# A three-layer fp32 model on one core: a new order for two merged attentions, and two weight-split steps moved

## What is computed

```python
# even mixer, after the projections; 8 heads each, causal, 512 tokens
mla = softmax(mask(q @ k.T * 96**-0.5)) @ v            # q, k of 96 columns, v of 64
z   = sq @ sk.T * 64**-0.5                             # stick-breaking, 64 columns
lb, l1 = log_sigmoid(z), where(k_idx < q_idx, log_sigmoid(-z), 0)
a   = where(k_idx < q_idx, exp(lb + reverse_cumsum(l1) - l1), 0)
sb  = a @ sv
o   = concat(mla, sb) @ w_o
```

## Time and profile before

| what | value |
|---|---|
| median of three runs | 2888.7 us |
| the profiled execution | 2887.3 us |
| its span | 2885.6 us |
| mean granted clock of TensorE in it | 0.939 |
| TensorE, VectorE, ScalarE, GpSimd busy | 2657.8, 1522.2, 1234.1, 122.6 us |

### The profile page before, as it was taken

One profiled execution on the slowest core, in us unless ns is written; L12 is line 12 of the kernel. 1 busy time (PEld: TensorE's weight loads), 2 busy tenths in 40 slices (PEclk: granted clock), 3 DMA queues, 4 the chain that ended last, 5 costly groups with the idle time before them and its releaser, 6 DMA issues. The chain is left out here.

```text
span 2885.6 us, 30599 instructions
## 1 busy us (share of the span) xinstructions
PE 2657.8 (92%) x12110; PEld 2158.0 (75%) x12110; DVE 1522.2 (53%) x2085; ACT 1234.1 (43%) x1570; POOL 122.6 (4%) x166
## 2 busy tenths in 40 slices
PE   6998999999998999999989969798995899999994
PEld 5866778888887777888877658677874777877774
DVE  4555444344323654434466443245346788888884
ACT  3366432223334742213222222324242677777773
POOL 0111000000140000000000000000002000000001
PEclk9967799999998999999989989899997899999997
DMA  3300132433431023342322022221304899999993
GB/s 130 119 1 1 50 120 93 139 109 119 138 110 37 1 76 116 108 146 88 117 88 88 30 95 88 73 88 59 142 14 190 345 392 396 395 396 396 396 392 119
DMA packets 157146, 432.84 MB, mean 150 GB/s; under 512 B 11051, under 2 KB 80838, under 8 KB 144582
## 3 DMA queue, kind: packets, MB, share of 16 engines
q1 hardware_dynamic: 148950, 400.90, 38.1%
q10 hardware_dynamic: 4608, 16.78, 1.4%
q0 software_dynamic: 3440, 13.11, 1.3%
HBM read 383.58 MB, written 47.19 MB: 149 GB/s over the span
## 5 line engine op out<-in xcount | busy, mean ns | idle before, releaser
L307 PE MATMUL ps<-area,area 128*128 128x512 f32 (+1 forms) x1696 | 658.5, 388 | 0.0
L330 DVE TENSOR_TENSOR area<-area,area 128x2048 fp32r<-128x2048 f32 (+4 forms) x161 | 340.5, 2117 | 598.5 <-ACT area L324 598.5
L306 PE MATMUL ps<-area,area 128*128 128x512 f32 (+5 forms) x1432 | 552.0, 385 | 0.0
L324 ACT ACTIVATE area<-area 128x2048 fp32r<-128x2048 f32 (+4 forms) x161 | 284.1, 1767 | 615.6 <-PE ps L307 582.4
L2324 DVE TENSOR_TENSOR area<-area,area 128x2048 fp32r<-128x2048 f32 x192 | 433.9, 2286 | 107.3 <-ACT area L2319 107.3
L305 PE MATMUL ps<-actT_parts,area 128*128 128x512 f32 x968 | 385.4, 398 | 11.6 <-DVE area L330 9.4
L306 PE MATMUL ps<-actT_parts,area 128*128 128x512 f32 x968 | 383.3, 396 | 0.0
L2319 ACT ACTIVATE area<-area 128x2048 fp32r<-128x2048 f32 x192 | 361.0, 1913 | 48.5 <-PE ps L2353 18.4
L307 PEld LDWEIGHTS ps<-area,area 128*128 128x128 f32 x1696 | 320.4, 189 | 68.3
L306 PEld LDWEIGHTS ps<-area,area 128*128 128x128 f32 x1432 | 277.5, 194 | 52.8
L305 PE MATMUL ps<-area,actT_parts 128*128 128x512 f32 (+3 forms) x704 | 274.6, 390 | 39.6 <-DVE area L330 30.8
(11 more groups left out here) (329 smaller groups left out, 3205.3 us busy)
## 6 DMA issues: line engine op xcount, KB each, us to landing
area<-in_w SPq DMA_DIRECT2D x96, 2048.0 KB, 10.1
area<-in_w_in SPq DMA_DIRECT2D x16, 2048.0 KB, 7.9
area<-in_l_w_gate SPq DMA_DIRECT2D x22, 1024.0 KB, 5.4
area<-in_l_w_up SPq DMA_DIRECT2D x22, 1024.0 KB, 8.0
expert_inputs<-maskz SPq DMA_DIRECT2D x39, 512.0 KB, 8.7
area<-in_l_w_in SPq DMA_DIRECT2D x9, 2048.0 KB, 8.2
area<-expert_inputs SPq DMA_DIRECT2D x32, 512.0 KB, 9.7
expert_rows<-area ACTq DMA_DIRECT2D x32, 512.0 KB, 8.6
```

The source lines that it names most:

```text
L306: pe.matmul(dst(r), a.l, b.h, start=False, stop=False)
L307: m = pe.matmul(dst(r), a.h, b.l, start=False, stop=end)
L324: eng.activation(w.h, raw, ACT.Copy).then_inc(w_hi, 1)
L330: dve.tensor_tensor(w.l, raw, w.high_f, ALU.subtract).then_inc(w_lo, 1)
```

## The change

No arithmetic is added or removed.

- In the merged attention the methods of class `Attention` are cut into steps (`pe_preps`, `pe_scores`, `pe_turn`, `pe_values`; `act_preps`, `act_copy`, `act_exp`; `dve_out`), as are those of stick-breaking, and the four loops call them in a new order. Iteration v now is, on TensorE: stick-breaking transposes of v - 3, its scores v, MLA preparations, stick-breaking values v - 5 (before v - 4), MLA scores v, MLA transposes v - 2, MLA values v - 4 (before v - 3). On ScalarE: absolute value and exponential v, copy v - 3, weights' exponential v - 2, logarithm v, MLA preparation copy, MLA copy v - 2, MLA exponential v. On VectorE: MLA output v - 5 (before v - 4), scan v - 1, stick-breaking output v - 5, subtraction v - 1, MLA maximum and bias v, stick-breaking log step v. On GpSimd: triangle of the weights v - 2 (before v - 1), triangle of the sums v.
- MLA has one score bank (0) in place of two, stick-breaking three (1, 3, 4) in place of two. `prep_bank` and `turn_banks` are not changed, both are bank 2. The wait of stick-breaking's scores for the subtraction of unit v - 2 is not changed.
- In the mixer `after` stands behind a job's second chunk.
- In the experts `turned_low` stands at q = p + 1.

The Fox and mLSTM attentions call the cut methods in the old order.

```diff
             def pe(self, pe, v):
+                self.pe_preps(pe, v)
+                self.pe_scores(pe, v)
+                self.pe_turn(pe, v - 2, v)
+                self.pe_values(pe, v - 3)
...
             mla = Attention(...
-                            score_banks=(0, 1), turn_banks=(2,), value_banks=(6,), prep_bank=2)
+                            score_banks=(0,), turn_banks=(2,), value_banks=(6,), prep_bank=2)
...
             def sb_bank(v):
-                return ps[:, 3 + v % 2, 0:causal(v)]
+                return ps[:, (1, 3, 4)[v % 3], 0:causal(v)]
...
             def two_po(po, ch):
-                for v in range(U0 + 1):
...
+                for v in range(U0 + 2):
+                    drop_weights(po, v - 2)
+                    drop_sums(po, v)
 
             def two_pe(pe, ch):
-                for v in range(U0 + 4):
-                    sb_pe(pe, v)
-                    mla.pe(pe, v)
+                for v in range(U0 + 5):
+                    sb_turn(pe, v - 3)
+                    sb_scores(pe, v)
+                    mla.pe_preps(pe, v)
+                    sb_values(pe, v - 5)
+                    mla.pe_scores(pe, v)
+                    mla.pe_turn(pe, v - 2, v)
+                    mla.pe_values(pe, v - 4)
 
             def two_act(act, ch):
                 act.preload_act_table_set("natural_log_exp_and_others")
                 for v in range(U0 + 3):
-                    sb_act(act, ch, v)
-                    mla.act(act, v)
+                    t1 = T1[:, v % 4, 0:causal(v)]
+                    if v < U0:
+                        act.wait_ge(b_sc, v + 1)
+                        if v >= 4:
+                            act.wait_ge(b_w, v - 3)
+                        ch(act.activation(t1, sb_bank(v), ACT.Abs))
+                        ch.mark(act.activation(t1, t1, ACT.Exp, scale=-1.0))
+                    powers = ch.n
+                    sb_copy(act, v - 3)
+                    sb_weights(act, v - 2)
+                    if v < U0:
+                        ch.wait(powers)
+                        act.activation(t1, t1, ACT.Ln, bias=1.0).then_inc(b_t1, 1)
+                    mla.act_preps(act, v)
+                    mla.act_copy(act, v - 2)
+                    mla.act_exp(act, v)
 
             def two_dve(dve, ch):
                 for v in range(U0 + 5):
-                    sb_dve(dve, ch, v)
+                    mla.dve_out(dve, ch, v - 5)
+                    sb_scan(dve, ch, v - 1)
+                    scanned = ch.n
+                    sb_out(dve, v - 5)
+                    sb_less(dve, ch, v - 1, scanned)
                     mla.dve(dve, ch, v)
+                    sb_logs(dve, v)
...
@@ mp_act, and the same in mp_dve @@
-                    if c % 4 == 3:
+                    if c % 4 == 1:
                         msp.after(act, at_qk[j])
...
@@ ex_dve @@
-                        if q == p + 2:
+                        if q == p + 1:
                             turned_low(dve, n)
```

More of the change, by code:

```diff
@@ L880, in pe, with pe_scores @@
                         m.then_inc(s_pr, 1)
-                if self.mlstm and v < units and v % NT == 0:
+            def pe_scores(self, pe, v):
+                nsc = len(self.sc_banks)
+                if self.mlstm and v < self.units and v % NT == 0:
                     if v:
@@ L943, in act, with dve_out @@
                                        accum_out=col(rs, v)).then_inc(s_ex, 1)
[L945 to L949, removed]
+            def dve_out(self, dve, ch, u):
+                if 0 <= u < self.units:
                     h, i = divmod(u, NT)
@@ L954, in dve @@
                     dve.tensor_scalar(self.dst(h, i), self.value_at(u), col(rinv, u), None, ALU.mult).then_inc(s_on, 1)
-                    last = False
+            def dve(self, dve, ch, v):
+                units, mlstm, length = self.units, self.mlstm, self.length
+                last = 4 <= v < units + 4 and len(self.vb) > 1
                 if v < units:
@@ L1459, in sb_pe, with sb_values @@
                     m.then_inc(b_pt, 1)
-                if 4 <= v < U0 + 4:
-                    u = v - 4
+            def sb_values(pe, u):
+                if 0 <= u < U0:
                     h = u // NT
@@ L1470, in sb_pe, with sb_weights @@
                     m.then_inc(b_o, 1)
[L1472 to L1482, removed]
+            def sb_weights(act, u):
+                if 0 <= u < U0:
                     act.wait_ge(b_m2, u + 1)
@@ L1492, in sb_act, with sb_scan, sb_less, sb_logs @@
                     act.activation(PT2[:, u % 2, 0:L], ps[:, 5, 0:L], ACT.Copy).then_inc(b_pe, 1)
-            def sb_dve(dve, ch, v):
-                if 5 <= v < U0 + 5:
-                    u = v - 5
+            def sb_scan(dve, ch, u):
+                if 0 <= u < U0:
+                    L = causal(u)
+                    dve.wait_ge(b_m1, u + 1)
+                    if u >= 4:
+                        dve.wait_ge(b_pt, u - 3)
+                    ch.mark(dve.tensor_tensor_scan(Pb2[:, u % 4, 0:L][:, ::-1], ones[:, 0:1].to_broadcast([P, L]),
+                                                   T1[:, u % 4, 0:L][:, ::-1], 0.0, ALU.mult, ALU.add))
+            def sb_less(dve, ch, u, scanned):
+                if 0 <= u < U0:
+                    p = Pb2[:, u % 4, 0:causal(u)]
+                    ch.wait(scanned)
+                    dve.tensor_tensor(p, sb_bank(u), p, ALU.subtract).then_inc(b_w, 1)
+            def sb_logs(dve, u):
+                if 0 <= u < U0:
+                    dve.wait_ge(b_t1, u + 1)
+                    t1 = T1[:, u % 4, 0:causal(u)]
+                    dve.scalar_tensor_tensor(out=t1, in0=sb_bank(u), scalar=0.0, in1=t1,
+                                             op0=ALU.max, op1=ALU.add).then_inc(b_sp, 1)
+            def sb_out(dve, u):
+                if 0 <= u < U0:
                     h, i = divmod(u, NT)
@@ new lines, in drop_weights @@
+            def drop_weights(po, u):
+                if 0 <= u < U0:
+                    dg = Pb2[:, u % 4, causal(u) - P:causal(u)]
+                    po.wait_ge(b_w, u + 1)
+                    po.affine_select(out=dg, in_=dg, compare_op=ALU.is_gt, fill=NEG,
+                                     base=0, pattern=[[-1, P]], channel_multiplier=1).then_inc(b_m2, 1)
+            def two_po(po, ch):
+                for v in range(U0 + 2):
+                    drop_weights(po, v - 2)
+                    drop_sums(po, v)
```

70 lines of the change are left out of this document (27 added, 43 removed).

## The result

| | us | against before, 95% interval |
|---|---|---|
| before, median of 7 in the same set | 2888.4 | |
| after, median of 7 | 2898.6 | 1.0036 [1.0024, 1.0047] |
| predicted | 2850.7 | |

The account below looks back on a forecast made before the run. It took TensorE, busy 92% of the span with clock dips and waits, as the bound. Experts 17.0, mixer 10.5, merged attention 7.5 and drain 3.0 made 38.0 us: 2850.7 from 2888.7, range 2827 to 2870.

Parts of the forecast that it names:

- Experts: Experts: low half ready before TensorE wants it, 0.55 us an expert over 31 experts, 17.0 us gained.
- The rival that transfers hold the period: Experts: transfers hold them at 18.6 us each; total gain 21, 2868 us; chance 0.07.
- Mixer: Mixer: earlier weight split shrinks the stop from 8.6 to 1.7 us and removes a second one; 10.5 us gained.
- Merged attention: Merged attention: clock goes on changing, heads of 19.5 instead of 20.6 us; 7.5 us gained.
- rival (d): Merged attention: clock stays at 1.2 GHz throughout, heads of 25.4 us, kernel slower at 2896 us; chance 0.04.
- the stop that I named as the example: Merged attention before the change: clock said to fall behind the wait at 220.27, 256-column scores then taking 1.22 us.
- The walks: Merged attention, new order worked through at each clock level: 16.6 us a head at 2.4 GHz, 25.4 at 1.2.
- Drain: End of the merged attention, 19.8 us at the low level: 3 us gained.
- Rival (e): Merged attention: no bank for preparations despite the change's name, already in the sum; something undoing the rest, about 2889, chance 0.03.
- my ring: Merged attention: new cycle from ScalarE's exponential v - 1 through TensorE's steps to exponential v; 16.6 us a head at 2.4 GHz.
- Rival (b): Merged attention gains nothing or loses some, single score bank making TensorE wait; heads 20.6 to 22, 2861 to 2870; chance 0.24.
- the middle case: Whole kernel: merged attention's clock stays a mix of both levels, heads of 19.5 us; forecast 2850.7 us, chance 0.45.

Follow-up runs that it names:

- e2: Kernel before with only the mixer's and the experts' edits, its merged attention untouched: 2861.3 us, 0.9901 of before.
- e7: Changed kernel, stick-breaking on banks 1 and 3, two unused products (64 rows, 512 columns) added before MLA's transposes in each preparation iteration: 2959.6 us.
- e5: e3 with one wait put back, MLA's transposes waiting for ScalarE's preparation copies: 2897.8 us, 1.0033 of before.
- e3: Changed kernel with MLA's preparations in a bank of their own (4) and stick-breaking on banks 1 and 3: 2806.9 us, 0.9721 of before.
- e12: e3 with the wait of e5 put back from iteration 16 on only: 2860.0 us.
- e14: Changed kernel with MLA's score products over 128 rows instead of 96, the last 32 zeros written by VectorE: 2850.7 us, 0.9867 of before.
- e10: As e7, but with eight unused 128 x 128 transposes added in each preparation iteration instead of the two products: 2833.0 us.
- e13: e9 with one added product instead of two in each preparation iteration: 2835.6 us, 0.9828 of before.
- e17: The kernel of e3 unchanged, run again with more executions: 2820.0 us, 0.9759 of before.
- e4: Changed kernel in its new order with two score banks for MLA (0 and 1) and two for stick-breaking: 2894.8 us, 1.0023 of before.
- e9: The kernel of e7 with the two added products over 128 rows instead of 64: 2839.9 us.
- e11: Changed kernel with ScalarE's preparation copy moved ahead of the stick-breaking weights' exponential and the logarithm: 2887.2 us.
- e6: e3 with the other wait put back, MLA's preparations waiting for the copy of the unit before: 2815.3 us, 0.9743 of before.

## Why the prediction was wrong

**Experts.** Right in place and mechanism: the wait is gone, VectorE waits 0.43 us (I said 0.4), no engine waits for a load, 407 GB/s as worked out. The size was 15.2 for 17.0, or 0.49 us an expert: I had added 0.1 for the restart to a gap of 0.45, and it cost half of that. The rival that transfers hold the period fell.

**Mixer.** Right. The stop went from 8.8 to 1.85 us between starts, 6.95 gained for 6.9; the low stretch and the second stop went too. From the norm's row to the experts 9.7 (e2) to 12.2 us (after) were gained, for 10.5; what makes the difference between the two stays open.

**Merged attention: the step that failed.** "So I expect it to go on changing. With half of the time low ... I take 19.5." The clock did not change; it was 0.50 throughout, rival (d), to which I gave 0.04. What I wrote against it, that at the low level the order comes almost without a gap and that today's clock rises in this stage, were both true and did not carry: TensorE was recorded busy 94% and no rise came, and in e7 none came at 100% either. I had taken a mean over two levels, where it had to be asked which of them this order can enter and which it can leave. In its place the runs show one wait: with it the stage stays at 0.50 and 27.0 us a head (e5), without it the clock goes to 1.00 and a head takes 13.6 us (e3). The stop behind the copy can end the high level: e12 lost it at the first one, e14 at the fourth. Why the level, once low, is not left again with these stops stays open; the rows in use seem to be part of it (e14).

I had also misread the stop that I named as the example. Behind the wait that ends at 220.27 the scores of 128 columns still take 0.48 us, as at the high level. The level fell at the end of the next stop, which I left out (clock 1.00 from 222 to 223, 0.76 to 224, then 0.50):

```profile
223.76 1.09 PE L907 MATMUL ps<-area,area 128*128 128x64 f32 x4 [1.43 <-DVE actT L954]
```

Length alone doesn't tell, though: in the same trace the level falls again at about 237.5, behind a stop of only 0.74 us that ended at 234.91.

The walks themselves were near. At the high level with the shared bank I had 16.6 us a head; e10, e13 and e14 show 16.9 to 17.0. At the low level I had 25.4, measured 27.0. TensorE's work was the term: 22.9 by my count, 25.1 by e7 (32.5 less two times 3.71 of added products), mainly since the score products cost more in the stream than 1.71 us for 512 columns: 2.00 for stick-breaking's (193.98 to 195.98 in e7) and 1.81 for MLA's (197.31 to 199.12), so the end that I took to be hidden is paid at least in part. A head's score products take 10.2 us by their starts in the changed kernel (from 320.06 on), where I had 8.6; the rest of the 2.2 was not worked out. The stops were 1.8 for my 2.4. With the first and the last head shorter than 27.0 (25.8; 4.75, 5.2 and 5.6 us an iteration in the last, which has no preparations), the stage lost 33.8 where (d) had 35; (d) gave 2896, and 2898.6 was measured.

**Drain.** 2.5 us gained for 3; the clock rose only at about 348, and averages 0.64 over the drain.

**The bank.** I read the diff rightly: the preparations got no bank, although the change is called so, and wrote that this was "already in the sum". In the sum it stood as 2.3 us a head of waits. It was worth 78 to 91 us (e5 against e17 and e3), because beside the waits it decides the clock. Rival (e) should have been worked out the other way round: what would the new order do with the bank that its name promises? With the copy out of the transposes' way my ring gives 16.6 less 2.3, 14.3 us, near the 13.6 of e3.

**Rival (b)** named the single score bank as the danger; e4 puts it at about 4 us at the low level. The range ended at 2870, since 0.04 was all I left for the low level.

The Trainium skill ("TensorE: Matmul & The Clock Gate", A second HAM failure mode), cited for the middle case, tells of a clock that goes on changing. The kernel before does that; the changed kernel does not, with a stop in two iterations of four it stays low.

## What to carry to other kernels

Where TensorE's clock is a mix in a stage, don't scale the mean: work out the stage at each level, and look in the trace for what stood before each fall and each rise. Two kernels that differ in one wait (e5 and e3), which stops TensorE 1.2 and 0.6 us in two of four iterations, lay 78 to 91 us apart. The PSUM bank that two steps of TensorE share here made it wait for whatever stood in ScalarE's queue ahead of the copy; a bank taken from a place where it buys nothing (here the third one of stick-breaking) removes it. And a new order and a new bank can each be worth nothing or less alone and much together, so both have to be priced together.

## What the runs showed of the hardware

TensorE can be recorded busy 219.6 of 220 us and be granted 0.50 all the time (e7). Products of the same columns over 128 rows instead of 64 brought 1.00 (e9, e13), and MLA's scores over 128 rows instead of 96, the added ones zeros, brought the kernel's own schedule from 0.50 to 0.74 (e14). So in these kernels the granted clock went with the rows that the products use, although rows do not change a product's recorded time at a given level: e14's MLA product of 512 columns takes 2.02 us with 128 rows at the low level, and so does the 96-row one of the changed kernel at 261.64. The Trainium skill ("TensorE: Matmul & The Clock Gate", What's actually happening) says that the clock goes by how busy the PE has been recently. e9 agrees; e7 agrees only if busy means something else than the record's busy time. How the chip weighs rows was not measured, and whether the values in the added rows matter was tried only with zeros (e14).

With eight added transposes, over 128 rows too, the stage also had the high level (e10, one execution: 1.00 from 180 to 280). The Trainium skill ("TensorE: Matmul & The Clock Gate", Part 4: PE-mode transpose) says that transposes do not engage the full clock, since they don't count as busy in the same way. In e10 the clock rises within the eight (0.50 from 167 to 168, 0.92 from 168 to 169), but they stand right behind wide products, so it does not show that they raise it alone; and they leave stops of 0.83 and 0.44 us a head, through which the level holds.

That the clock, once low, can stay low for long is seen in e11 (0.50 from 160 to 320) and in e12 (0.50 from 222 to 300). Why e6 and e12 reached the high level some 26 us later than e3, in the same order of work, stays open, and so does why e14 lost it at its fourth stop, of 1.32 us, when it had held through 1.64, 1.32 and 1.70.
